# Query projection as a 2x2 block product, one gate difference placed ahead of the queries' norm, and the pooling branch's sums in another tile

## The reference, cut to what matters

```python
proj = rms_norm(x, norm1_g) @ w_in
q, k, v, qi, ki, wi, pool_in, gate_a, gate_p = jnp.split(proj, split_at, axis=-1)   # q: 512 columns
q = rope(rms_norm(q.reshape(b, s, 8, 64), q_norm_g), positions)
attn = dsa_attention(q, k, v, qi, ki, wi)            # top 64 keys of each query
pooled = multiscale_pool(pool_in, pool_mix_w, pool_scale)
merged = (jax.nn.sigmoid(gate_a) * (attn @ w_branch_attn)
          + jax.nn.sigmoid(gate_p) * (pooled @ w_branch_pool))
x = x + merged @ w_out
x = x + moe_ffn(rms_norm(x, norm2_g), router_w, ...)  # top 4 of 32 experts, 12 MB of weights each
```

## Time and profile before

| | us |
|---|---|
| median of 3 executions | 1086.28 |
| lowest and highest of them | 1085.93, 1089.0 |
| profiled execution, its own time | 1087.07 |
| profiled execution, span of the profile | 1085.1 |
| TensorE busy in the span | 1048.3 (97%) |
| VectorE busy in the span | 390.3 (36%) |
| ScalarE busy in the span | 123.5 (11%) |
| mean rate of the transfers | 397 GB/s |

### The profile page before, as it was taken

One profiled execution on the slowest core, in us unless ns is written; L12 is line 12 of the kernel. 1 busy time (PEld: TensorE's weight loads), 2 busy tenths in 40 slices (PEclk: granted clock), 3 DMA queues, 4 the chain that ended last, 5 costly groups with the idle time before them and its releaser, 6 DMA issues.

```text
span 1085.1 us, 12201 instructions
## 1 busy us (share of the span) xinstructions
PE 1048.3 (97%) x4826; PEld 424.4 (39%) x4826; DVE 390.3 (36%) x721; ACT 123.5 (11%) x218; POOL 15.3 (1%) x31
## 2 busy tenths in 40 slices
PE   9999999999999999999998989899989999898998
PEld 6445445344343434343333324243434333332432
DVE  3798885123232322232322222223222322232222
ACT  3115213100000001000000000000000000000001
POOL 4000000000000000000000000000000000000000
PEclk9999999999999999999999999899999999999999
DMA  9914599999999999999999999999999999999996
GB/s 330 365 43 156 198 426 362 417 430 410 427 429 427 429 429 433 428 433 428 429 432 429 429 427 432 431 432 432 432 431 428 435 430 429 431 431 426 428 426 268
DMA packets 37064, 430.44 MB, mean 397 GB/s; under 512 B 4224, under 2 KB 6400, under 8 KB 16432
## 3 DMA queue, kind: packets, MB, share of 16 engines
q1 hardware_dynamic: 35328, 427.59, 93.5%
q0 software_dynamic: 1136, 1.91, 0.5%
q10 hardware_dynamic: 576, 0.60, 0.2%
HBM read 429.03 MB, written 1.05 MB: 396 GB/s over the span
## 4 chain that ended last, share of the span: by engine, by line
PE 73%; DMA 24%; DVE 1%; issue 1%; SPq 1%; ACT 0%; ACTq 0%; DVEq 0%
PE bank L1673 30%; DMA ring<-w_gate_up_dram 24%; PE bank L1702 14%; PE bank L1598 5%; PE bank L1393 5%; PE bank L1254 4%; PE bank L1625 4%; PE bank L1691 2%; PE bank L1552 2%; PE bank L1271 2%; PE bank L1218 1%; PE bank L1651 1%; PE bank L1727 1%; PE bank L1277 0%; SPq L315 0%
## 5 line engine op out<-in xcount | busy, mean ns | idle before, releaser
L1673 PE MATMUL bank<-ring,scr 128*64 128x512 f32 x2032 | 476.4, 612 | 27.3 <-DMA ring<-w_gate_up_dram 27.2
L1673 PEld LDWEIGHTS bank<-ring,scr 128*64 128x64 f32 x2032 | 141.1, 140 | 325.7 <-issue 285.5
L1702 PE MATMUL bank<-ring,scr 128*64 128x512 f32 x992 | 225.0, 595 | 0.0
L1158 DVE TENSOR_TENSOR x<-bank,x 128x512 f32<-128x512 f32 x120 | 77.3, 686 | 255.4 <-PE bank L1625 255.4
L1702 PEld LDWEIGHTS bank<-ring,scr 128*64 128x64 f32 x992 | 68.9, 137 | 127.3 <-issue 123.2
L1133 DVE COPY scr<-bank 128x512 f32<-128x512 f32 x32 | 22.1, 692 | 257.6 <-PE bank L1673 257.6
L1139 DVE TENSOR_TENSOR scr<-bank,bgu 128x512 f32<-128x512 f32 x64 | 41.2, 686 | 98.5 <-PE bank L1691 98.5
L1625 PE MATMUL bank<-scr 64*128 64x512 f32 x240 | 67.7, 641 | 0.1
L589 ACT ACTIVATE scr<-bank 128x512 f32<-128x512 f32 x32 | 19.1, 598 | 383.4 <-PE bank L1673 383.4
L1598 PEld LDWEIGHTS bank<-scr,xn 128*128 128x128 f32 x480 | 54.8, 192 | 13.0 <-issue 13.0
L1598 PE MATMUL bank<-scr,xn 128*128 128x128 f32 x480 | 57.8, 278 | 0.0
(11 more groups left out here) (231 smaller groups left out, 534.1 us busy)
## 6 DMA issues: line engine op xcount, KB each, us to landing
ring<-w_gate_up_dram SPq DMA_DIRECT2D x40, 4096.0 KB, 31.8
ring<-w_down_dram SPq DMA_DIRECT2D x62, 2048.0 KB, 17.5
ring<-w_gate_up_dram SPq DMA_DIRECT2D x40, 2048.0 KB, 19.7
ring<-w_gate_up_dram SPq DMA_DIRECT2D x13, 1024.0 KB, 8.4
ring<-w_in_dram SPq DMA_DIRECT2D x12, 1024.0 KB
ring<-w_out_dram SPq DMA_DIRECT2D x4, 1024.0 KB
ring<-w_down_dram SPq DMA_DIRECT2D x4, 1024.0 KB, 28.0
ring<-w_branch_pool_dram SPq DMA_DIRECT2D x2, 1024.0 KB
```

The costliest lines, as they stand in the source:

```text
L1158: V.tensor_tensor(x[:, b, 512 * h:512 * h + 512], XY[h][:, :], x[:, b, 512 * h:512 * h + 512], ALU.add).then_inc(read[f"Y{j}"], 1)
L1673: ins = MM(GB[h][T * g:T * g + T, :], xgT[:, k, T * e:T * e + T], w[:, c0:c0 + 512], start=k == 0, stop=k == KC - 1)
L1702: ins = MM(DB[T * h:T * h + T, :], actT[e][:, c, :], v3(dn_slot[j][:, :], 4)[:, k, 512 * h:512 * h + 512], start=c == 0, stop=c == KC - 1)
```

## The change

It has four parts.

1. `projection(2)` goes. In its place stands `query_projection`, a 2x2 block product like those of the gates: seven products of four matmuls with 256 columns each. Its left sides are the blocks a11, a12, a22 and the sums s1 to s4 that are there already. VectorE makes four differences of the queries' weights (`query_part`): three before the second half of the keys' work, the fourth after the keys' root. Four of the products add up in bank 4, which ScalarE copies out after each (`query`, 128x256); the other three lie in banks 5, 3 and 2, and VectorE adds them in (`query_add`, four of them). The first gate now waits for `query_added`.
2. `part(0, 2)` moves ahead of the queries' norm, and the norm's and the rotation's temporaries move from `ptb` to `half[4]`.
3. The pooling branch's sums `pool_s` move from `half[5]` to `kqT_t`, which nobody reads after the attention scores. The attention branch's sums lie there too, and now wait for the pooling branch's seventh product.
4. On SP, unit 23 is loaded ahead of the first two `load_gu`, and unit 22 after the fifth product of the pooling branch rather than the seventh; `load_gu(4, 1)` and `load_gu(7, 1)` get the wait for the seventh.

```diff
-        pool_s = [v3(half[5][:, 256 * i:256 * i + 256], 2) for i in range(4)]
+        pool_s = [v3(kqT_t[:, 256 * i:256 * i + 256], 2) for i in range(4)]
+        query_w = [v3(half[u], 4)[:, :, 256 * h:256 * h + 256] for u in (4, 5) for h in range(2)]
+        query_t1, query_t2 = v3(siga_t[:, 0:1024], 4), v3(siga_t[:, 1024:2048], 4)
+        query_out = [qq[:, b, 256 * h:256 * h + 256] for b in range(NB) for h in range(2)]
...
             for u in range(1, PRE_UNITS - 2):
                 pre_unit(u)
+            sp.wait_ge(prod_done, N_PROD + 3)
+            sp.wait_ge(part_ready[1], 4)
+            pre_unit(PRE_UNITS - 1)
...
-            sp.wait_ge(block_prod, BLOCK_PROD)
-            for u in range(PRE_UNITS - 2, PRE_UNITS):
-                pre_unit(u)
+            sp.wait_ge(block_part, POOL_P + BLOCK_PART)
+            sp.wait_ge(block_prod, POOL_M + BLOCK_PROD - 2)
+            pre_unit(PRE_UNITS - 2)
             sp.wait_ge(t_ready, TJ_O + 2)
             load_gu(2, 0)
             load_gu(3, 2)
+            sp.wait_ge(block_prod, POOL_M + BLOCK_PROD)
             load_gu(4, 1)
             load_gu(7, 1)
...
+            def query(product, i, b, signal, n):
+                act.wait_ge(block_prod, product)
+                nc.scalar.activation(query_out[i], bank[4][:, 0:256], ACT.Copy, scale=small[:, 128 + b:129 + b]).then_inc(signal, n)
+
+            query(1, 0, 0, block_copied, 1)
             root(132, 6, 2)
-            job(2, qq)
+            query(3, 2, 1, block_copied, 1)
+            query(5, 3, 1, block_copied, 1)
+            query(7, 1, 0, job_read, 2)
...
+            def query_part(i):
+
+                w11, w12, w21, w22 = query_w
+                out, a, b = [(query_t1, w12, w11), (w12, w22, w12), (query_t2, w22, query_t1), (w11, w21, query_t2)][i]
...
+            for i in range(3):
+                query_part(i)
...
             root_and_reciprocal(132, 6, 1.0 / HD, 2)
+            query_part(3)
...
             part(0, 0)
             part(0, 1)
+            part(0, 2)
+            query_add(0, 0, bank[5], 2, 1, 0)
+            query_add(3, 1, bank[3], 5, 3, 0)
+            query_add(2, 1, bank[3], 5, 2, 0)
+            query_add(2, 1, bank[2], 6, 2, 3)
+            dve.wait_ge(query_added, 4)
             dve.wait_ge(job_read, 6)
-            head_squares(q4, HEADS, 140)
+            dve.wait_ge(block_prod, BLOCK_PROD)
+            head_squares(q4, HEADS, 140, half[4])
...
-            part(0, 2)
             part(1, 0)
...
+            dve.wait_ge(block_prod, POOL_M + 7)
             for i in range(4):
                 att_sums(i)
-            dve.wait_ge(block_prod, 7)
             gated(0, 1, bank[4][:, :])
...
+                unit(4)
+                product(bank[4], a11, w11, True)
+                unit(5)
+                product(bank[5], a12, w21, True)
+                pe.wait_ge(block_copied, 1)
+                pe.wait_ge(sums_ready, 4)
+                pe.wait_ge(block_part, 3)
+                product(bank[4], s2, query_t2, False)
+                pe.wait_ge(job_read, 4)
+                product(bank[3], s3, t3, True)
+                pe.wait_ge(block_copied, 2)
+                product(bank[4], s1, query_t1, False)
+                pe.wait_ge(block_part, 4)
+                product(bank[2], a22, t4, True)
+                pe.wait_ge(block_copied, 3)
+                product(bank[4], s4, w22, False)
...
                 if g == 0:
-                    pe.wait_ge(job_read, 4)
+                    pe.wait_ge(query_added, 4)
```

More of the change, by code:

```diff
@@ L294, in unit_free @@
                 if u < 8 and u % 2 == 1:
-                    sp.wait_ge(job_ready, u + 1)
+                    sp.wait_ge(job_ready, u + 1 if u < 4 else u - 1)
                 elif u < 8:
@@ L487, in job @@
                 for b in range(NB):
-                    act.wait_ge(job_ready, 2 * j + b + 1)
+                    act.wait_ge(job_ready, 2 * (j if j < 2 else j - 1) + b + 1)
                     n = groups[j][1]
@@ L558, in _ @@
             tcopy(TJ_O, attnT[:, :, 0:P])
-            copy_block(0, 5, bank[4], att_u4)
+            copy_block(POOL_M, 5, bank[4], att_u4)
             tcopy(TJ_O + 1, attnT[:, :, P:2 * P])
@@ L680, in _, with rope @@
             sin = v3(sin_t, NB)
-            def rope(src, outs, nh, half, stride):
+            def rope(src, outs, nh, half, stride, tmp=ptb):
                 cb = cos[:, :, ::stride].unsqueeze(2).to_broadcast([P, NB, nh, half])
@@ L686, in rope @@
                 x1, x2 = src[:, :, :, 0:half], src[:, :, :, half:2 * half]
-                t = [r[:, 0:NB * nh * half].rearrange("p (b h n) -> p b h n", b=NB, h=nh) for r in rtmp]
+                t = [tmp[:, 512 * j:512 * j + NB * nh * half].rearrange("p (b h n) -> p b h n", b=NB, h=nh) for j in range(4)]
                 V.tensor_tensor(t[0], x1, cb, ALU.mult)
@@ L722, in _, with query_add @@
             V.tensor_tensor(s4, a12, s2, ALU.subtract).then_inc(sums_ready, 1)
+            def query_part(i):
+                w11, w12, w21, w22 = query_w
+                out, a, b = [(query_t1, w12, w11), (w12, w22, w12), (query_t2, w22, query_t1), (w11, w21, query_t2)][i]
+                if i == 0:
+                    dve.wait_ge(unit_in[4], 16)
+                else:
+                    dve.wait_ge(block_part, i)
+                if i == 1:
+                    dve.wait_ge(unit_in[5], 16)
+                elif i == 3:
+                    dve.wait_ge(block_prod, 1)
+                V.tensor_tensor(out, a, b, ALU.subtract).then_inc(block_part, 1)
+            def query_add(i, b, acc, product, copied, before):
+                dve.wait_ge(block_prod, product)
+                dve.wait_ge(block_copied, copied)
+                if before:
+                    dve.wait_ge(query_added, before)
+                V.scalar_tensor_tensor(out=query_out[i], in0=acc[:, 0:256], scalar=small[:, 128 + b:129 + b], in1=query_out[i],
+                                       op0=ALU.mult, op1=ALU.add).then_inc(query_added, 1)
+            for i in range(3):
+                query_part(i)
             def part(g, i):
@@ L1296, in _, with query_projection, product @@
             projection(0, lambda: turn_x(1))
-            for j in range(1, 4):
-                projection(j)
+            projection(1)
+            def query_projection():
+                w11, t3, w21, w22 = query_w
+                t4 = w11
+                def product(acc, lhs, rhs, fresh):
+                    for k in range(4):
+                        ins = MM(acc[:, 0:256], lhs[:, k, :], rhs[:, k, :], start=fresh and k == 0, stop=k == 3,
+                                 skip_group_check=not fresh)
+                    ins.then_inc(block_prod, 1)
+                unit(4)
[14 more added lines that the diff above has]
+                product(bank[4], s4, w22, False)
+            query_projection()
+            projection(3)
             def turn_k():
```

44 lines of the change are left out of this document (23 added, 21 removed).

## The result

The kernel after takes **1089.64 us** (median of 22 runs, 1086.99 to 1091.72); the kernel before, in 22 runs, 1087.15 us (1085.93 to 1089.0). The ratio is 1.0022, with a 95% interval of 1.0016 to 1.0027: 2.5 us slower where the prediction had 1.2 us faster. The spans of the two profiles say the same, 1087.5 against 1085.1 us.

What follows compares the result with a forecast made beforehand. Experts' weight transfers bound the last stage, so only TensorE's arrival there counts: 0.3 us earlier after the scores plus 0.9 at the merges gives 1.2 us, a median of 1085.1 us, range 1082.5 to 1088.0.

Steps and rivals of the forecast that it cites:

- TensorE's own saving: Queries' projection: sixteen 512-column matmuls (13.8 us) give way to 28 of 256 columns (12.0 us), saving 1.8 us.
- VectorE's side, early: Before 38.44 us: keys' work ends 3.4 us later, hidden by a 4.14 us wait; 0.7 us of cover left.
- VectorE's side, from 38 us: From 43.27 us to the scores VectorE never waits; four new adds make it 1.7 us later.
- Where they meet: At the attention scores VectorE's lateness costs TensorE most of its lead, leaving it 0.3 us earlier than before.
- The 1.1 and 0.4 us at the scores: TensorE waits 1.1 us for VectorE's reads of two banks, then loses 0.4 more to the fourth gate sum.
- The rival on the other side: VectorE becomes the head's bound, TensorE paying its extra lateness one for one: 1086 to 1087 us; chance 0.15.
- a broken cover, dearer adds: Early cover of 0.7 us breaks, or the adds cost 2.6 us: 1 to 2 us more are lost.
- The loads: Units 23 and 22 issued earlier; the merges' waits shrink, leaving TensorE 1.2 us earlier in all.
- the wait for `w_out`: VectorE's 1.37 us wait for unit 23 at `out_part(1)`, before 139.83 us, goes.
- the hole in the stream: The transfers' 7 us lead becomes a hole between 161 and 168 us, as `w_down` still waits.
- the 1.1 us of the merges: TensorE's 1.10 us wait for VectorE at 146.28 goes nearly whole, a gain of 0.9 us.
- The end of the kernel moves by as much as TensorE's arrival at the experts moves: Last stage: with all ten slots full, only TensorE's arrival at the experts moves the end; nothing else in the head counts.

Runs made afterwards that it cites:

- e1: Kernel after with the first gate's first sum moved from behind VectorE's first top 64 into its third round; 1086.14 us, ratio to before 0.9995.
- e4: Kernel before with parts 3 and 4 of the change alone (pooling sums' tile, order of loads); 1085.88 us, ratio to before 0.999.
- e5: e1 without parts 3 and 4 of the change (pooling sums and SP order as before); 1085.88 us, ratio to before 0.999.
- e13: Kernel before, its four dead start matmuls replaced by fourteen small ones (40 instructions more on TensorE); 1086.21 us, ratio 0.9989.
- e10: e5 run again unchanged for another trace; 1086.38 us in a single time.
- e7: e1 with the second query block's attention scores later and the first gate's fourth sum in the second top 64; 1084.89 us, ratio to before 0.9982.
- e14: Kernel before, its four dead start matmuls replaced by eight small ones (16 instructions more on TensorE); 1087.64 us in a single run.
- e3: Kernel after with the first gate's third difference moved back behind the queries' norm and rotation; 1088.62 us, ratio to before 1.0013.
- e2: Kernel before with a dead VectorE multiply of about 2.3 us ahead of the second gate's first difference; 1089.56 us, ratio 1.0024.
- e6: Kernel after with six dead 256-column matmuls on TensorE ahead of the wait in which it stopped; 1087.78 us, ratio to before 1.0008.
- e8: Kernel before run again unchanged for another trace; 1086.44 us in a single time.
- e9: Kernel before run once more unchanged for another trace; 1087.45 us in a single time.
- e11: Kernel before with 40 already-met waits added on TensorE behind the first matmuls; 1087.3 us, ratio 1.0001.
- e12: Kernel before with 12 already-met waits added on TensorE behind the first matmuls; 1087.73 us in a single run.

## Why the prediction was wrong

- **TensorE's own saving**, 1.8 us: right. The gate starts at 50.37, 1.82 us earlier, and the records stand 0.215 us apart (56 of them from 24.56 to 36.6 us) with no wait in them.
- **VectorE's side, early**: right. Three differences end near 27.2 us, and `part(0, 0)` starts at 38.33 with 1.22 us of wait left, where I had 0.7.
- **VectorE's side, from 38 us**: right in size. The four adds take 1.88 us (0.47 each; I had 1.7), and VectorE starts the indexer's scores at 65.94, 1.9 us later than the 64.05 of before.
- **Where they meet: this is the step that failed.** "From 43.27 us on it has no wait for anyone up to the attention scores" is true of VectorE but for 0.28 us for ScalarE at 46 us, and I took it as if TensorE had no wait for VectorE either. It had one, for the first gate's first sum, with 0.6 us of slack at 72.4 to 73.00. The two shifts that I had worked out, 1.9 and 1.8 us, add up to 3.7 there; less 0.6 that is 3.1, and the stop is 3.04. Both shifts were in the prediction, and the place was not: I looked for waits that show as waits, and this one had never been late. The 1.1 and 0.4 us at the scores did not come about, because VectorE itself waited there for TensorE for 2.33 us; in e1, where the stop is gone, the 1.1 came as forecast, at 1.15.
- **The clock** was no term at all: it was put at nothing without a reason, and was 1.7 us by the trace. No case of mine had TensorE idle for longer than 1.1 us at a time.
- **The rival on the other side** (VectorE as the bound of the head) was the nearest, and had the direction. It had the price wrong: it took VectorE's lateness one for one and wanted some of it beyond the reckoned 1.7 us (a broken cover, dearer adds) before anything was lost. Here the reckoned lateness itself, 1.9 us, went with a loss of 2.25 at the experts and 2.5 by the medians, as TensorE's earliness counts in the same wait and the clock comes on top.
- **The loads**: the wait for `w_out` went, and the hole in the stream came, at 166 to 170 us rather than 161 to 168. Unit 23 was issued at 111.12 us rather than near 105, unit 22 at 128.67 rather than near 126. In the kernel after, the 1.1 us of the merges only paid back part of the loss: TensorE came to the scores 3.1 us late, the wait of 1.10 us was not there, and the 2.0 that are left are its lateness at 148.32. Taken alone the loads are worth 1.1 us (e4: medians 1085.88 against 1087.01). Beside parts 1 and 2 they are worth nothing that the times show (e5 against e1). By e13 the likely reason is that the 48 instructions of twelve more matmuls had already moved the code packet out of unit 23's way: it comes at 126 us in e5 and e10. So the term was right for the kernel before, and was counted as the loads' alone when the query product had it too.
- **"The end of the kernel moves by as much as TensorE's arrival at the experts moves"**: right in every run. After: 2.25 and 2.4 us. e1, e4, e5, e7 and e13 start the experts 1.1 to 2.3 us earlier, and their medians lie 0.7 to 2.1 us under before's.

The sum with the missed step in it: -1.8 + 3.04 + 1.7 = +2.9 at the scores, less the 1.1 of the merges is +1.8, where 2.0 were measured at 148.32 and 2.25 at the experts. With one sum moved (e1) the change is level with before, 0.9 us lower by the medians and with an interval that spans 1; with the scores moved too (e7) it is 2.1 us under. It lost by one wait.

## What to carry to other kernels

When one engine gets earlier and another later, add the two shifts and hold the sum against **every** point where the first waits for the second, those too that show no wait now; their slack is the time between the releasing instruction's end and the waiting one's start, and has to be read from both timelines. A stop on TensorE is then priced with what the clock takes behind it, and a filler or an earlier producer is tried before the change is given up. And a gain that is read from one late load should be tried by itself: a piece of code that happens to be fetched in that load's way may be its cause, and then an unrelated edit that shifts the program can give the same (e13), or fail to (e14).

## What was not expected of the hardware

- In the traces, the granted clock stood at 0.50 for some 3.4 us behind a stop of 3.04 us (after) and behind one of 2.58 us (e3); behind one of 2.37 us (e2), and behind 0.52 us with filler ahead of it (e6), it stayed at 1.00. What was busy ahead of these stops differed too, and each is one execution, so no bound is read from four cases. Nor need the fall come in every execution: of the 22 runs of the kernel after, the four fastest (1086.99 to 1087.99 us) have a mean granted clock of 0.985 to 0.986, the other 18 (1088.62 to 1091.72) of 0.982 to 0.985. Those four may have stopped without the fall; none of them was traced.
- A packet of the queue "q8 instruction", which moves with TensorE's program (e13), takes time among the weights' transfers. With this one packet of 16 KB, 0.9 us of one engine, in the middle of a stream at some 400 to 430 GB/s, the load in that stream landed 1.1 to 1.5 us later: waits of 1.28 to 1.73 us in seven profiles with the packet at 136 to 139.3 us and the old order of loads (before, e2, e8, e9, e11, e12, e14), and of 0.20 to 0.32 us in three (e5, e10, e13) with it at 125 to 127.
